# One weight block, two streams of 256 columns, one merged order of steps for all engines

## The reference

```
for l in range(2):                                  # block 1
    p = rms_norm(x) @ w_in                          # 1024 -> 2832
    y_a = conformer_conv(...)                       # gated, 31 taps, layer norm, silu
    y_b = head_norm(causal attention, 4 heads)      # one block of 256 keys
    y_c = head_norm(gated linear attention, chunks of 32) * silu(r)
    x = x + concat(y_a, y_b, y_c) @ w_out
    u = conv3(rms_norm(x) @ w_up)                   # 1024 -> 2 x 2816, 3 taps over tokens
    x = x + (silu(u_1) * u_2) @ w_down              # 2816 -> 1024
x = rms_norm(x)
for l in range(2):                                  # block 2, x and h_ctx alike, but for "last" layer
    mod = silu(c) @ w_ada + b_ada                   # 9 x 1024, for x and for h_ctx
    x, h_ctx = half step of a swiglu FFN on each (same weights)
    q, k, v = modulate(rms_norm(.)) @ w_in          # q, k normed by head, half of them rotated
    x     += attention of 16 heads over 256 local keys (bias table or window) and 256 context keys
    h_ctx += attention of 16 heads over the 256 context keys      (not in the last layer)
    x, h_ctx = half step of a swiglu FFN            (h_ctx not in the last layer)
```

## Time and profile before

| | |
|---|---|
| median of the runs | 3066.08 us |
| the profiled execution's own time | 3061.71 us |
| its span, first to last instruction | 3059.9 us |
| TensorE, VectorE, ScalarE, GpSimd busy | 2657.5, 1617.6, 1050.3, 77.2 us |
| mean granted TensorE clock | 0.889 |
| read from memory | 347.85 MB |

### The profile page before, as it was taken

How to read it: one execution, slowest core, us unless ns; L and a number is a source line. 1 busy time by engine, 2 the same in 40 slices (tenths; PEclk the granted TensorE clock), 3 DMA queues, 4 the chain that set the end, 5 groups by cost and what they waited for, 6 DMA issues and landing times.

```text
span 3059.9 us, 39437 instructions
## 1 busy us (share of the span) xinstructions
PE 2657.5 (87%) x15612; PEld 2312.5 (76%) x15612; DVE 1617.6 (53%) x2580; ACT 1050.3 (34%) x1422; POOL 77.2 (3%) x149
## 2 busy tenths in 40 slices
PE   6678889579889999999656899999999998865999
PEld 5578889479787888879533678887788888844999
DVE  4757888558865565742443345744333334333554
ACT  3335634246534222231233233122331223123553
POOL 0000000000000000000000000000000000000000
PEclk9769999579989999998786789999899998768999
DMA  5324574135552453521000124532222222100454
GB/s 211 109 96 159 193 260 152 69 111 192 191 195 103 146 191 137 179 83 42 1 1 1 56 90 144 200 131 90 76 89 98 98 94 90 35 1 1 145 183 147
DMA packets 98005, 350.80 MB, mean 115 GB/s; under 512 B 10577, under 2 KB 13777, under 8 KB 97617
## 3 DMA queue, kind: packets, MB, share of 16 engines
q1 hardware_dynamic: 77136, 273.43, 25.4%
q0 software_dynamic: 20736, 75.51, 7.2%
HBM read 347.85 MB, written 1.05 MB: 114 GB/s over the span
## 4 chain that ended last, share of the span: by engine, by line
PE 73%; DVE 16%; ACT 7%; issue 3%; DMA 0%; SPq 0%; ACTq 0%; DVEq 0%
PE half L508 19%; PE half L510 19%; PE half L509 19%; PE half L619 3%; DVE PROD L1068 2%; PE half L627 2%; DVE U L1403 2%; ACT PR L904 2%; PE half L589 2%; DVE W_lo L1079 2%; PE half L564 2%; ACT W_hi L865 2%; DVE PR L1171 1%; PE half L842 1%; PE half L554 1%
## 5 line engine op out<-in xcount | busy, mean ns | idle before, releaser
L1079 DVE TENSOR_TENSOR W_lo<-W_raw,W_hi 128x1024 fp32r<-128x1024 f32 x510 | 622.5, 1224 | 868.2 <-ACT W_hi L865 866.6
L508 PE MATMUL half<-H_hi,W_lo 128*128 128x256 f32 (+1 forms) x2848 | 961.4, 338 | 57.6 <-DVE H_lo L1131 19.0
L509 PE MATMUL half<-H_lo,W_hi 128*128 128x256 f32 (+1 forms) x2848 | 951.8, 334 | 0.0
L510 PE MATMUL half<-H_hi,W_hi 128*128 128x256 f32 (+1 forms) x2848 | 951.0, 334 | 0.0
L865 ACT ACTIVATE W_hi<-W_raw 128x1024 fp32r<-128x1024 f32 x510 | 536.8, 1058 | 1162.2 <-PE half L510 1092.2
L508 PEld LDWEIGHTS half<-H_hi,W_lo 128*128 128x128 f32 x2848 | 550.9, 193 | 126.8 <-issue 28.9
L510 PEld LDWEIGHTS half<-H_hi,W_hi 128*128 128x128 f32 x2848 | 551.8, 194 | 50.5
L509 PEld LDWEIGHTS half<-H_lo,W_hi 128*128 128x128 f32 x2848 | 552.7, 194 | 48.6
L508 PE MATMUL half<-HID_hi,W_lo 128*128 128x256 f32 (+1 forms) x1056 | 356.6, 338 | 19.9 <-DVE W_lo L1079 17.5
L509 PE MATMUL half<-HID_lo,W_hi 128*128 128x256 f32 (+1 forms) x1056 | 356.0, 337 | 0.0
L510 PE MATMUL half<-HID_hi,W_hi 128*128 128x256 f32 (+1 forms) x1056 | 356.0, 337 | 0.0
(11 more groups left out here) (166 smaller groups left out, 2215.8 us busy)
## 6 DMA issues: line engine op xcount, KB each, us to landing
W_raw<-wstream SPq DMA_DIRECT2D x510, 512.0 KB, 3.2
A_raw<-adastream POOLq DMA_DIRECT2D x144, 512.0 KB, 3.6
CON<-const SPq DMA_DIRECT2D x1, 1025.5 KB, 8.7
X<-xT SPq DMA_DIRECT2D x1, 1024.0 KB, 5.7
X<-ctxT SPq DMA_DIRECT2D x1, 1024.0 KB, 14.8
SC<-cond SPq DMA_DIRECT2D x1, 1024.0 KB, 11.1
outT<-X SPq DMA_DIRECT2D x1, 1024.0 KB, 4.8
PAR<-par SPq DMA_DIRECT2D x1, 684.0 KB, 11.0
```

The costliest lines, as they stand in the source:

```text
L508: pe.matmul(out, wl, xh, start=start, stop=False, skip_group_check=True)
L509: pe.matmul(out, wh, xl, start=False, stop=False, skip_group_check=True)
L510: return pe.matmul(out, wh, xh, start=False, stop=stop, skip_group_check=True)
L1079: dve.tensor_tensor(W_lo[:, v % RING, :], W_raw[:, v % RING, :], W_hi[:, v % RING, :].bitcast(F32), ALU.subtract).then_inc(S.w_lo, 1)
```

## The change

The program is written anew around two streams, A (image) and B (context), of 256 columns each, with tensors, PSUM slots, counters and semaphores of their own.

- Each stream is a list of stages, each stage a list of steps; a step either uses one weight unit or none (`G`). `make_order` merges the two lists into one order of visits. A may be up to three units ahead of B; B uses the same split unit after A. Block 1 and the last layer's part without context have A alone ("solo").
- Every engine (SyncE too) runs through that one order; its functions are generators that do this engine's share of a step and yield.
- Weight unit: 24 matmuls of 256 columns for each stream that needs it. `W_lo` is written over `W_raw`; ring of 6 for these, of 4 for `W_hi`; splits still three units ahead.
- PSUM is four slots of two banks; a solo stage uses four, in joint stages each stream has two.
- The steps of attention, gates and norm sums are put between weight units: in `mix1` (in1, att1 and out of block 1 together), in `in2` (sums and spreads of q and k), in `out`.
- The root is a power on GpSimd instead of Ln and Exp on ScalarE. Squares and the last update of X are made in halves or quarters.
- The bias table is written by GpSimd's DMAs, 128 per layer, during an earlier FFN. Conditioning loads are issued by SyncE, ring of 2; steps are placed by `place_ada`: 24 in block 1's down parts, the other 120 one per shared unit in the FFNs of layer 0 of block 2.
- The last columns of V come from a transposed copy of a feature-wise product.
- Attention groups: two per stream in flight. Joint: `probs_t(i), weighted(i), scores(i+2)`, alternating A and B; solo: `probs_t(i), weighted(i-1), scores(i+2)`.
- Loads at the start have semaphores of their own; the store is in three parts. No rolled loops.
- New placement in SBUF: H, HID and X start 64 or 128 bytes past round addresses.

```diff
+RAW = 6
+HIGH = 4
 AHEAD = 3
+LAG = 2
...
+    def b_may():
+        if ib >= len(b): return False
+        u = b[ib].unit
+        if u is None: return True
+        if u not in open_units: return False
+        ahead = len(open_units) - open_units.index(u) - 1
+        return ahead >= LAG or ia >= len(a) or a[ia].unit is None or a[ia].unit not in shared
+    def a_may():
+        return ia < len(a) and (a[ia].unit is None or len(open_units) <= (LAG if a[ia].unit in shared else 0)) \
+            and not (a[ia].stage.solo and ib < len(b)) \
+            and not (a[ia].stage.kind == "att2" and ib < len(b) and b[ib].stage.kind == "in2")
+    while ia < len(a) or ib < len(b):      # each turn: one step of A if it may, one of B if it may
...
+        for s, h_at, x_at, arena in ((A, 40 * K + 64, 150 * K + 128, AA), (B, 56 * K + 64, 158 * K + 128, AB)):
+            s.H_hi = at("H_hi" + n, h_at, [P, KT, SEQ], F32R)
+            s.HID = at("HID" + n, arena, [P, 6, 2, 512], F32R)
...
+            def root(s, rs, n):            # GpSimd
+                pool.wait_ge(s.sem.var, rs + 1)
+                pool.tensor_tensor(s.R0[:, 0:n], s.V_[:, 0:n], EXPO[:, 0:n], ALU.pow).then_inc(s.sem.r0, 1)
+            def bias_table(l):
+                for c in range(64):
+                    for h in range(2):
+                        pool.dma_start(BT[64 * h + c:64 * h + c + 1, c0:c0 + 16, :], rows[h:h + 1, r:r + 16, :])
...
+            def att2(s, st):               # TensorE
+                for i, g in enumerate(gs):
+                    probs_t(s, st, g); yield
+                    if i >= behind: weighted(s, st, gs[i - behind])
+                    yield
+                    if i + 2 < len(gs): scores(s, st, gs[i + 2])
+                    yield
...
+            for v in ORDER:                # VectorE; the other engines alike
+                if v.final: split(v.g + AHEAD)
+                if v.i == 0: at_step[v.s] = table[v.stage.kind](streams[v.s], v.stage)
+                next(at_step[v.s])
+                for _ in range(v.ada): ada()
```

More of the change, by code:

```diff
@@ new lines, in make_plan, with add, ffn @@
+def make_plan():
+    blocks = []
+    total = dict(u=0)
+    def add(kind, units, **kw):
+        blocks.append(Block(kind, units, total["u"], **kw))
+        total["u"] += units
+    def ffn(l, blk, groups, which=0):
+        for a, b in groups:
+            add("up", 4 * (b - a), l=l, blk=blk, m0=a, pairs=b - a, ffn=which)
+            add("down", 2 * (b - a), l=l, blk=blk, m0=a, pairs=b - a, ffn=which)
+    whole = ((0, PAIRS),)
+    for l in range(DEPTH):
+        add("in1", 23, l=l)
+        add("out", 8, l=l, blk=1)
+        ffn(l, 1, whole)
+    for l in range(DEPTH):
+        ffn(l, 2, GROUPS, 0)
+        add("in2", 18, l=l)
+        add("out", 8, l=l, blk=2)
+        ffn(l, 2, whole if l == DEPTH - 1 else GROUPS, 1)
+    return blocks, total
@@ new lines, in out2, with end @@
+            def out2(s, st):
+                pe.wait_ge(s.sem.evac, st.tok)
+                yield from out_units(s, st, st.tok, range(8), None)
+            def end(s, st):
+                yield
+            table = dict(norm=norm, final=final, mix1=mix1, ffn=ffn, in2=in2, att2=att2, out2=out2, end=end)
+            pe.wait_ge(S.con_in, 16)
+            pe.wait_ge(S.par_in, 16)
+            pe.wait_ge(S.at_zero, 1)
+            at_step = {}
+            for v in ORDER:
+                now.visit = v
+                if v.i == 0:
+                    at_step[v.s] = table[v.stage.kind](streams[v.s], v.stage)
+                next(at_step[v.s])
@@ L1039, in att2 @@
[L1039 to L1051 removed]
+                act.activation(s.H_hi[:, 0:2, :], s.TMP[:, 0:2, :], ACT.Copy).then_inc(S.mix_hi, 1)
@@ new lines, in plain @@
+            def plain(s, st):
+                for _ in st.steps:
+                    yield
+            table = dict(norm=norm, final=final, mix1=mix1, ffn=ffn, in2=in2, att2=att2, out2=plain, end=plain)
+            for g in range(AHEAD):
+                split(g)
+            at_step = {}
+            conditioned = False
+            for v in ORDER:
+                if v.final:
+                    split(v.g + AHEAD)
+                if v.i == 0:
+                    at_step[v.s] = table[v.stage.kind](streams[v.s], v.stage)
+                next(at_step[v.s])
+                if not conditioned and v.stage.kind == "mix1":
+                    act.wait_ge(S.cond_in, 16)
+                    act.activation(SC[:, :, :], SC[:, :, :], ACT.Silu).then_inc(S.cond_ready, 1)
+                    conditioned = True
@@ L1524, in _constants @@
+            for g in range(AHEAD):
+                split(g)
+            at_step = {}
+            for v in ORDER:
+                if v.final:
+                    split(v.g + AHEAD)
+                if v.i == 0:
+                    at_step[v.s] = table[v.stage.kind](streams[v.s], v.stage)
+                next(at_step[v.s])
+                for _ in range(v.ada):
+                    ada()
 def _constants():
```

2699 lines of the change are left out of this document (1604 added, 1095 removed).

## The result

The changed kernel takes 2,900.68 us (median of 4 runs, 2,895.01 to 2,903.61) against 3,064.94 us (4 runs) before: ratio 0.946, interval 0.9442 to 0.9479. The forecast was 2,752 us with a range of 2,650 to 2,865, so it is faster as said, but by 164 us and not 313. The profiled execution took 2,903.61 us, its span 2,901.7.

A forecast was written before the change was run, and what follows sets the result against it. The prediction took TensorE as the bound: full FFNs set by matmul pace, attention and norms by waits and low clock that interleaving could cover. Its terms summed to -309 us from a 3,059.9 us span, forecasting 2,752 us, range 2,650 to 2,865.

The forecast's parts named there:

- The step that failed: Joint norms: context units beside the image's norm, about 16 us lost per pair of norms, -13 us for four.
- What is left is TensorE's own: Block 2's projections with query-key norm: TensorE's work and few waits, 128 us in layer 0, 99 in layer 1, together -98.
- I take 1 us: Norms: the root as GpSimd's power, which no row shows, between nothing and the 3.5 us it replaces.
- I take the middle, 0.1167 us for H: Joint FFNs: 256-column matmuls on H at 0.1167 us, giving 365.6 us per FFN, three worth -1 us (-20 to +22).
- Groups: Block 2's attention: 16 alternating pairs in layer 0 take 190 us, -31; layer 1's image-only groups stay at 141.40, 0 us.
- Mixers: Block 1's mixer with projection and output: 155 us per layer for 190.80, -36 each, -72 together; ends 140 and 175.
- Final norm with norm 0: Final norm with the first norm of block 2: from 36.40 to 31 us, -5.
- slower than before: Rival: VectorE becomes the bound in the joint FFNs; at 8.3 us per unit the kernel takes 3,088 us; chance 0.05.
- the sign I had named: Sign that the forecast holds: mean clock above 0.92.
- All hides: Rival: H at 0.113 us, groups at full clock and mixers at 145 give 2,645 us; chance 0.2.
- the one order stalls: Rival: engines wait in each other's order, norms and groups overlap little; 2,865 us; chance 0.23.
- the two neighbours: The rivals at either end of the range: all hides, 2,645 us, chance 0.2; the one order stalls, 2,865 us, chance 0.23.

The follow-up runs named there:

- e9: LAG = 0 in place of 2 in the changed kernel: the context stream takes each shared unit right behind the image stream, with no lead; 2,850.19 us.
- e13: The changed kernel with layer 0's next attention group normalised ahead of a later group's maximum, and its probabilities copied ahead of the exponentials; 2,861.42 us.
- e7: The changed kernel with scores and maximum of group i+2 placed before the weighted sum of group i-1 in layer 1's image-only attention; 2,863.93 us.
- the best version: The changed kernel with LAG = 0, 192 bytes of distance, layer 1's scores first, layer 0's normalisation early and the mixer's first group early; 2,723.24 us.

## Why the prediction was wrong, point by point

**The step that failed** is "In the new order the image's norm has two or three context units beside it (2.7 us each), the context's stands right behind", and with it "What is left is TensorE's own" for the projection. I counted what TensorE had to do beside the norm and took the lead for its cover. At a joint norm what decides is VectorE's place for the context's update: with a lead of two it stands behind the image's scalings (1195.98, the product done at 1190.4), with a lead of one ahead of them. In layer 0's projection three terms were short. Waits were 4 and measured 22.0 us, since VectorE stands behind GpSimd's root and TensorE behind VectorE; sums and spreads were 23 and measured 31; the weight matmuls were 101 and measured 113, since a part of them ran at half clock. Joint norms and projections missed 90 us. With LAG = 0 the profiled execution is 52 us shorter: 17 at the joint FFNs with their norms, 25 at the projections, 7 at output and norm of layer 0, 6 at layer 1's groups, less 3 at layer 0's groups. Some 40 of the 90 are not won back by it.

**A size that was off: the root.** "I take 1 us", within 0 to 3.5. It is 0.70 for a norm, but 2.90 us for 16 columns, a shape that I did not look up in the projection, where the tail waits for it twice. All powers doubled cost 43 us. The tails (sums, power, spread of 3.7 us) remain in the projections; e9 still has 145.6 us for the 128 forecast.

**The pace.** "I don't know; I take the middle, 0.1167 us for H", HID at 0.113. Both ran at 0.1178: in the FFNs 9,504 matmuls on H x 1.1 ns and 4,752 on HID x 4.8 ns are 33 us, of the 39 that all FFNs missed. The reason named, that H and HID would stand alike at plus 64, was half right: the address decides and not the order of PSUM, but what counts is the distance to the weights. HID's 0.1133 belonged to 192, and the change put it at 64. The Trainium skill (TensorE: Matmul & The Clock Gate, Back-to-back issue gap) has a formula for the gap of single matmuls, which gives 109.2 ns for 256 columns. The trace doesn't agree: no pace here was below 113.3.

**Groups.** Layer 0 190 forecast, 174.4 measured; layer 1 141 and 147.3. The mechanism was right: the one order bound them, as e13 and e7 show by taking 37 us each out of them with the same work. The sum had a slip: its terms for a pair add up to 9.4 us at full clock and not 9.7, so 184 us and not 190. By the Trainium skill's rule (same page, Part 4: PE-mode transpose) that transposes don't count as work for the clock, the prediction estimated 13.5 us for a pair. A pair took 10.9 (174.4 / 16), there were as many transposes as before (192, not twice as many), and with the same transposes in less time the clock was 0.92. So the trace does not bear the rule out as the bound here.

**Mixers.** 155 forecast, 164 measured. I had 8 us for all of VectorE's waits; the wait before the first transposes alone is 10.6, because splits, taps and a maximum stand ahead of the first normalisation. Moving it won only 2.4 us, so most of the 9 us are elsewhere in the tail, and that is open.

**Final norm with norm 0.** 31 forecast, 40.5 measured. The forecast put no conditioning here, but the trace has three steps of it and the modulation's small sums on VectorE from 766.97 to 776.3, ahead of the last update of the image, while TensorE stands idle with half of its sums done:

```profile
776.30 1.28 DVE L1669 TENSOR_TENSOR XA<-slot,XA 128x512 f32<-128x512 f32 x2
777.70 3.58 PE L895 MATMUL slot<-CON,SQA 128*128 128x1 f32 x16 [7.56 <-ACT SQA L1317]
```

These 9.3 us are as much as was missed, but no run moves the three steps.

**What held.** FFNs of block 1 are bound by TensorE and not by VectorE (155.42 of 189.00 us busy). VectorE in the joint FFNs stays hidden at 275.52 of 372.90 us (about 280 of 366 forecast), so the rival "slower than before" fell. The bias table's DMAs stay beneath an FFN: 122.1 us of GpSimd for both, and no root behind them late; after the projection the scores follow at once. The mean clock did not pass 0.92, the sign I had named: it is 0.912. "All hides" (2,645) is not reached by the best version either. The rival "the one order stalls" came nearest: its mechanism is the right one, with 2,865 for 2,901, because I had given it the groups and mixers and not the norms.

**Why the range missed.** It held 0.43 of chance for the two neighbours, and each was priced as if the norms cost what I forecast. A kernel in which "every engine has its streams' steps in one queue" deserved the end at which nothing of a norm is hidden. With that end, +13 for the norms and +25 for each projection, the rival comes to 2,928, and 2,901 lies inside.

## What to carry to other kernels

When one static order serves all engines, price an overlap by the slowest hand-over in the order of *each* engine, not by what TensorE has left to do: here the small update of one stream stood behind eight steps of the other, and the lead, meant as cover, cost 50 us in all. Try the lead at 0, 1 and 2 before anything else is tuned, and put a step whose input has long been ready ahead of the one that waits. Look up where the two operands of a matmul lie against each other before a pace from one tensor is used for another, and give an op on a slow engine a price for its largest shape.

## What the runs showed of the hardware

- Back-to-back matmuls of 256 columns ran at 113.3, 117.8 or 120.0 ns from start to start at full clock when the moving operand lay 0, 64 or 192 bytes from the stationary one, modulo 256. At 0 it was 120.0; at 64 mostly 117.8 and at 192 mostly 113.3, and one burst can keep either for hundreds of microseconds. At 128 it was 120.0 or 118.5 to 118.8, at 224 118.3, in means over 24. With 512 columns it was 226.7 at distance 0 and 233.3 at 192: the other way round.
- GpSimd's power took 0.70, 1.01, 1.64 and 2.90 us for 2, 4, 8 and 16 columns, near 0.39 us and 0.16 us for each column.
- A stage with waits lost twice: when the waits before the transposes went, the granted clock rose from 0.81 to 0.92 and from 0.71 to 0.82, between the levels of 1.2 and 2.4 GHz.
- The 32 single-column sums took 3.6 to 4.9 us right behind a full unit, and 5.6 to 7.4 us behind an idle stretch or behind other sums.
